# Fourth feed-forward part: both parts of the activations in one matmul of 512 columns, bank halves added by VectorE

## Chip, cores and metric

One core of a Trainium2 chip runs the whole program in one launch. The metric is the device time in microseconds, from one execution; of several executions the median is taken. The inputs are float32.

## The reference, cut to what matters

The program computes two layers of a first network (feed-forward, mixer, feed-forward in each) on 256 latent and 256 context tokens, and then two layers of a second network on the 256 latent tokens. The change touches only the second feed-forward of layer 1, the fourth of the program, which has the latent tokens alone:

```python
D_MODEL = 1024; D_FF = 2816; MACARON_WEIGHT = 0.5

def swiglu(x, w_gu, w_down):
    gate, up = jnp.split(x @ w_gu, 2, axis=-1)
    return (jax.nn.silu(gate) * up) @ w_down

def ffn_sublayer(x, shift, scale, gate, w_gu, w_down, g, b):
    y = swiglu(modulate(x, shift, scale), w_gu, w_down)
    return deepnorm_residual(x, MACARON_WEIGHT * gate * y, g, b)   # layer_norm(ALPHA * x + ...)
```

## The kernel before

Activations lie transposed: partitions are features, 128 at a time (`KD` = 8 tiles of X, `KF` = 22 tiles of the hidden H), and columns are tokens, `T` = 512 in the first three feed-forward parts, `L` = 256 in the fourth.

A float32 product is made from operands of a rounded type (fp32r). Weights and activations are each split in two: an upper part, which is the value rounded by a copy on ScalarE, and a lower part, the rest, by a subtraction on VectorE or GpSimd. For each tile of 128 x 128 weights, three matmuls are added in one PSUM bank: upper weights by upper X (L1947), lower weights by upper X (L1948), upper weights by lower X (L1950). Each has its own load of weights into TensorE. With n = 256 a matmul has 256 columns, and only half of the bank is used.

Weights come in one stream from DRAM, in chunks of 1024 columns (512 KB), into a ring of three slots. Half a chunk, 512 columns or four tiles, is the unit of the split: ScalarE's `split_hi` (L2292, its copy is on L2296) and VectorE's `split_lo` (L2539, L2542) fill one of `NSPL` = 4 pairs of buffers in `spl`. `split_hi` of a half waits until TensorE has used the half that lay in the same buffer, four before. In the parts up to the second network VectorE makes all lower parts of weights; GpSimd makes those of H (`dual`, ScalarE's part on L2300, GpSimd's on L3023).

One generator, `order`, yields the steps of the whole program in one order, and each engine runs through it and emits those that it has a function for. So the queue of each engine is this order, and an instruction that waits holds all that follow on its engine. `take` (L357), called for each weight tile, starts a new half when one is used up, and `splits_ahead` (L374) then puts into the order the splits of the half three ahead. `linear` (L428) goes over the k tiles of one output; after each fourth tile (k % 4 == 3) it may pump a step of a background generator: in this part `ada_vec` (L2556, its instruction on L2566), 16 product-sums on VectorE for the modulation vectors of the last norm, which end before m = KF - 4. In each second of four tiles (k % 4 == 1) it takes one step from `trickle`, here the eight `ln_update` of ScalarE (L2358) that the norm before has left.

`ffn` (L818) first makes gate and up for m = 0 and 1 side by side, beside the norm (`side_by_side`). Then for m = 2 to 21 it calls `linear` for gate (8 tiles, two halves) and for up (8 tiles, two halves), and yields `glu`: ScalarE takes silu of the gate bank into a temporary tile (L2335), VectorE multiplies it by the up bank (L2626), and `dual` splits the product into H. The eight down outputs follow, of 22 tiles each, with `residual` (L2615): X + gate column times bank, on VectorE (L2620). A load of ScalarE's table for the square root stands between up and down.

Of the kernel before, what the change touches and what calls it, by code (L numbers as in the profile page):

```python
# [15 lines left out]
KD = D // 128  # L16
# [217 lines left out]
def build(nc, nch, W, PRM, CST, XT, MT, OUT, stage="all"):  # L234
    ctx = ExitStack()
    with ctx:
# [34 lines left out]
        def R(a, n):  # L271
            return bigr[:, a:a + n]

        def two(ap):
            return ap.rearrange("p (s t) -> p s t", s=2)
# [63 lines left out]
        def order():  # L339
# [87 lines left out]

            def linear(key, w, src, n):  # L428
                bank, free, bi = banks.get()
                for k, (hi, lo, need) in enumerate(src):  # L430
                    tile = yield from take(w(k))
                    yield "linear", key, bank, free, k, len(src), tile, (hi, lo), need, n
                    if k % 4 == 1 and trickle:
                        yield trickle.pop(0)
                    if k % 4 == 3 and pos["auto"]:
                        i, steps, of = pos["auto"]
                        pos["auto"] = i + 1, steps, of
                        yield from pump((i + 1) * steps // of - i * steps // of)
                yield from run_later()
                return bank, bi  # L440
# [261 lines left out]

            def residual(key, bank, bi, k, n, gate, sums, xneed):
                u = new()
                yield "residual", u, k, n, bank, gate[0], [key, gate[1]], xneed
                banks.give(bi, ("res_x", u))

                def squares():
                    return sums.add(Xt[k][:, 0:n], [("res_x", u)], k == KD - 1)

                if n == L and k < KD - 1:
                    later.append(squares)
                else:
                    yield from squares()
# [103 lines left out]
            def ffn(f, n, xs, ms, ln, nxt, early=(), late=(), free=()):  # L818
# [22 lines left out]
                for m in range(KF):  # L841
# [5 lines left out]
                    else:  # L847
                        (kg, ku), (wg, wu) = gate_up(m)
                        bg, ig = yield from linear(kg, wg, src, n)
                        bu, iu = yield from linear(ku, wu, src, n)  # L850
                    t, free, i = tmps.get()
                    yield "glu", f, m, t[:, 0:n], bg[:, 0:n], bu[:, 0:n], free
                    banks.give(ig, ("silu", f, m))
                    banks.give(iu, ("glu", f, m))
                    h = yield from dual(t[:, 0:n], H[m][0], H[m][1], [("glu", f, m)])
# [16 lines left out]
                for k in range(KD):  # L872
                    if f == 3 and k < 4:
                        yield from scaled_later(1, MN1, [("mem_v", 0)], (2 * k, 2 * k + 1), srcm)
                    b, bi = yield from linear(("down", f, k), tile_of("ffn_w_down", (l, j), 128 * k), [(H[m][0], H[m][1], [hs[m]]) for m in range(KF)], n)
                    yield from residual(("down", f, k), b, bi, k, n, gate, sums, xs[k])
                pos["auto"] = None
# [1045 lines left out]
        def tensor_program(pe, w):  # L1923
# [16 lines left out]
            def linear(key, bank, free, k, nk, tile, x, need, n):  # L1940
# [9 lines left out]
                finish(pe.matmul(out, hi, x[1], start=False, stop=k == nk - 1), tile, key if k == nk - 1 else None)  # L1950

            def linear_hi(key, bank, free, tile, x, need, n):
                w.all(free, done)
# [308 lines left out]
            def index_heads(l, heads, need, IDX):  # L2262
# [9 lines left out]
            run({f.__name__: f for f in (  # L2272
                tables, linear, linear_hi, linear_lo, by_token, ada, ada_raw, ada_turn, colsum, square_sum, warm, spread, gate_columns, tail_columns, turn_kv,
                gram, gate_rows, unit_turn, q_decay, level_p, level_u, u_values, w_keys, scan_v, scan_s, scan_own, head_turn,
# [3 lines left out]
        def scalar_program(act, w):  # L2278
# [49 lines left out]
            def first_scale(k):  # L2328
                w.wait_ge(*done("first_mod", k))
                act.activation(Xt[k], Xt[k], ACTF.Copy, scale=ALPHA).then_inc(*sig("x_scaled", k))  # L2330

            def glu(f, m, t, bg, bu, free):
# [163 lines left out]
            def index_heads(l, heads, need, IDX):  # L2496
# [5 lines left out]
            run({f.__name__: f for f in (  # L2502
                tables, start, cond_silu, split_hi, dual, evacuate, ada_row, square, root, deviation, sqrt_table, first_scale, glu, ln_mod, ln_shift, ln_update,
                gates_in, gates_exp, gates_ratio, short_conv, conv_silu, conv_glu, z_silu, tail_columns, turn_kv, decay, unit_turn, q_decay,
# [3 lines left out]
        def vector_program(dve, w):  # L2508
# [105 lines left out]

            def residual(u, k, n, bank, gt, need, xneed):  # L2615
                w.all(need, done)
                w.all(xneed, done)
                for s, a, b in halves(n):
                    x = Xt[k][:, a:b]
                    ins = dve.scalar_tensor_tensor(x, bank[:, a:b], gt[:, k, s:s + 1], x, MUL, ADD)  # L2620
                ins.then_inc(*sig("res_x", u))

            def glu(f, m, t, bg, bu, free):
# [373 lines left out]
            def final(k, r, key):  # L2997
# [4 lines left out]
            run({f.__name__: f for f in (  # L3002
                tables, start, split_lo, dual, ada_turn, ada_vec, ada_mod, acc_dve, moments, inverse, norm_cols, gate_cols, residual, glu, first_mod, ln_sub, ln_mul,
                ln_mod, alpha_cols, ln_gain, gates_in, gates_exp, gates_ratio, gates_series0, gates_series1, gates_series2, gates_scan, gates_back,
# [151 lines left out]
```

## Time and profile before

| | us |
|---|---|
| median of 3 runs | 2625.61 |
| lowest, highest | 2621.83, 2629.3 |
| profiled execution, its own time | 2627.34 |
| span of the profiled execution | 2625.6 |
| busy in the span: TensorE matmul | 2505.6 (95%) |
| weight loads into TensorE | 2172.5 (83%) |
| VectorE | 1728.2 (66%) |
| ScalarE | 1215.8 (46%) |
| GpSimd | 666.5 (25%) |
| granted TensorE clock, mean | 0.984 of full |

PE is TensorE's matmul, PEld its weight load (which goes on beside matmuls), DVE VectorE, ACT ScalarE, POOL GpSimd. The span runs from the first to the last instruction. Times in the rows below are microseconds from its start unless marked otherwise. L and a number is a line of the kernel. Matmul records overlap: what counts for the pace is the distance between their starts.

### The profile page before, as it was taken

The page shows a single profiled execution, that of the slowest core. Times are in us where ns is not written, and L with a number is a line of the kernel's source. Part 1 is how long each engine was busy: PE and PEld are TensorE (multiplying, and loading weights), DVE is VectorE, ACT ScalarE, POOL GpSimd, SP SyncE. Part 2 cuts the span into 40 slices and gives each one's busy share as a digit, 9 for nine tenths or more (in the row PEclk, how much of TensorE's full clock was granted, in tenths as well). Part 3 has the DMA queues.
Part 4 walks back from the last instruction along what each step waited for, and adds up shares of the span by engine and source line. Part 5 has one row for each costly group of instructions (what it writes and reads, how often), then busy time and mean ns, then how long its engine had stood idle before and what let it go on. Part 6 is the DMA issues. An engine that isn't in the chain of part 4 may idle for free.

```text
span 2625.6 us, 42978 instructions
## 1 busy us (share of the span) xinstructions
PE 2505.6 (95%) x16456; PEld 2172.5 (83%) x16456; DVE 1728.2 (66%) x3436; ACT 1215.8 (46%) x2307; POOL 666.5 (25%) x602
## 2 busy tenths in 40 slices
PE   8999999997879999999999999999999999999998
PEld 5777887886777887888888887789998899999998
DVE  5786487898876687356764456676663476746766
ACT  4223324752153523324433325656555568555684
POOL 1101022002313211112111122121135543655435
PEclk9999999998999999999999999999999999999999
DMA  7554352220001455433453442237544444444444
GB/s 276 173 188 150 138 186 89 73 88 10 3 1 65 168 177 176 137 132 124 157 176 133 156 147 74 97 105 246 192 158 144 138 152 145 169 145 145 153 137 145
DMA packets 119324, 359.05 MB, mean 137 GB/s; under 512 B 13136, under 2 KB 15312, under 8 KB 118736
## 3 DMA queue, kind: packets, MB, share of 16 engines
q1 hardware_dynamic: 119120, 356.30, 39.8%
q8 instruction: 131, 2.15, 0.3%
q14 instruction: 73, 0.60, 0.1%
HBM read 355.20 MB, written 1.05 MB: 136 GB/s over the span
## 4 chain that ended last, share of the span: by engine, by line
PE 71%; DVE 11%; ACT 6%; issue 4%; DMA 4%; POOL 2%; SPq 0%; DVEq 0%; POOLq 0%; ACTq 0%
PE ps L1947 20%; PE ps L1950 20%; PE ps L1948 19%; DMA ring<-w_stream 4%; ACT spl L2296 2%; DVE work L2566 2%; DVE spl L2542 1%; DVE big L2566 1%; PE ps L2011 1%; DVE big L2760 1%; PE ps L2204 1%; PE ps L1972 1%; PE ps L1974 1%; PE ps L1973 1%; PE ps L2241 1%
## 5 line engine op out<-in xcount | busy, mean ns | idle before, releaser
L1947 PE MATMUL ps<-bigr,spl 128*128 128x256 f32 (+1 forms) x3850 | 1310.3, 340 | 31.9 <-DVE spl L2542 23.7
L1950 PE MATMUL ps<-bigr,spl 128*128 128x256 f32 (+1 forms) x3850 | 1291.0, 335 | 3.4 <-POOL bigr L3023 3.1
L1948 PE MATMUL ps<-bigr,spl 128*128 128x256 f32 (+1 forms) x3850 | 1288.3, 335 | 0.0
L2542 DVE TENSOR_TENSOR spl<-ring,spl 128x512 fp32r<-128x512 f32 x838 | 659.5, 794 | 587.4 <-ACT spl L2296 583.8
L2296 ACT ACTIVATE spl<-ring 128x512 fp32r<-128x512 f32 x1024 | 629.3, 627 | 752.1 <-PE ps L1950 504.5
L1947 PEld LDWEIGHTS ps<-bigr,spl 128*128 128x128 f32 x3850 | 732.5, 190 | 130.7 <-DVE spl L2542 30.5
L1950 PEld LDWEIGHTS ps<-bigr,spl 128*128 128x128 f32 x3850 | 732.1, 190 | 84.3 <-POOL bigr L3023 10.2
L1948 PEld LDWEIGHTS ps<-bigr,spl 128*128 128x128 f32 x3850 | 733.0, 190 | 73.2 <-issue 1.7
L3023 POOL TENSOR_TENSOR bigr<-work,bigr 128x512 fp32r<-128x512 f32 (+1 forms) x200 | 209.3, 1050 | 920.0 <-ACT bigr L2300 919.8
L3018 POOL TENSOR_TENSOR spl<-ring,spl 128x512 fp32r<-128x512 f32 x186 | 252.4, 1358 | 275.7 <-ACT spl L2296 275.0
L2300 ACT ACTIVATE bigr<-work 128x512 fp32r<-128x512 f32 (+1 forms) x224 | 117.0, 525 | 263.1 <-DVE work L2626 167.3
L3027 POOL TENSOR_TENSOR work<-work,X 128x512 f32<-128x512 f32 (+1 forms) x36 | 40.9, 1135 | 227.3 <-DVE X L2620 227.3
L2566 DVE CUSTOM_DVE_ANT_0 big<-big,prm 128x512 f32<-128x512 f32 x128 | 97.2, 759 | 0.0
L2566 DVE CUSTOM_DVE_ANT_0 big<-big,small 128x512 f32<-128x512 f32 x128 | 97.2, 759 | 0.0
L2760 DVE SCALAR_TENSOR_TENSOR big<-big,prm 128x512 f32<-128x512 f32 x120 | 95.8, 839 | 0.0
L2626 DVE TENSOR_TENSOR work<-work,ps 128x512 f32<-128x512 f32 (+1 forms) x88 | 54.4, 618 | 41.4 <-PE ps L1950 27.7
L2566 DVE CUSTOM_DVE_ANT_0 work<-big,small 128x512 f32<-128x512 f32 x96 | 78.4, 817 | 0.0
L2315 ACT ACTIVATE work<-X 128x256 f32<-128x256 f32 (+1 forms) x72 | 36.3, 507 | 85.3 <-DVE X L2620 74.7
L3027 POOL TENSOR_TENSOR work<-work 128x512 f32<-128x512 f32 (+1 forms) x47 | 62.3, 1325 | 48.5 <-ACT work L2315 48.5
L2566 DVE CUSTOM_DVE_ANT_0 work<-big,prm 128x512 f32<-128x512 f32 x96 | 74.3, 774 | 0.0
L1972 PE MATMUL ps<-spl,bigr 128*128 128x512 f32 (+1 forms) x128 | 51.6, 403 | 1.6 <-DVE spl L2542 1.0
L2935 DVE TENSOR_TENSOR big<-big,work 128x256 f32<-128x256 f32 x52 | 30.4, 585 | 28.3 <-POOL big L3075 27.8
(312 smaller groups left out, 2377.9 us busy)
## 6 DMA issues: line engine op xcount, KB each, us to landing
ring<-w_stream SPq DMA_DIRECT2D x512, 512.0 KB, 3.3
big<-w_stream SPq DMA_DIRECT2D x280, 256.0 KB, 3.0
big<-w_stream SPq DMA_DIRECT2D x16, 512.0 KB, 10.8
X<-x_t SPq DMA_DIRECT2D x2, 1024.0 KB, 13.6
cst<-consts SPq DMA_DIRECT2D x1, 1537.5 KB, 9.0
X<-mem_t SPq DMA_DIRECT2D x1, 1024.0 KB, 5.9
out_t<-X SPq DMA_DIRECT2D x8, 128.0 KB, 2.1
prm<-params SPq DMA_DIRECT2D x1, 252.5 KB, 2.6
```

Of the source, the lines that this page charges most:

```text
L1947: pe.matmul(out, hi, x[0], start=k == 0, stop=False)
L1948: pe.matmul(out, lo, x[0], start=False, stop=False)
L1950: finish(pe.matmul(out, hi, x[1], start=False, stop=k == nk - 1), tile, key if k == nk - 1 else None)
L1972: pe.matmul(outs[i], src[0][:, a:b], hi, start=k == 0, stop=False)
L2296: act.activation(hi_half(h), raw_half(h), ACTF.Copy).then_inc(*sig("hi", h))
L2300: act.activation(hi, raw, ACTF.Copy).then_inc(*sig("dhi", u))
L2542: dve.tensor_tensor(lo_half(h), raw_half(h), hi_half(h), SUB).then_inc(*sig("lo", h, by="lo_dve"))
L2566: ins = dve.tensor_tensor_reduce(slot if s == conds - 1 else wk[7 + j % 2], slot, crow[s][h], 1.0, start, MUL, ADD, col)
L2760: ins = dve.scalar_tensor_tensor(two(CF[m]), YP[m][:, :, j:j + 256], a, two(CF[m]), MUL, ADD)
L3018: pool.tensor_tensor(lo_half(h), raw_half(h), hi_half(h), SUB).then_inc(*sig("lo", h, by="lo_pool"))
L3023: pool.tensor_tensor(lo, raw, hi, SUB).then_inc(*sig("dlo", u, by="dlo_pool"))
L3027: ins = pool.tensor_copy(dst, src) if copy else pool.tensor_tensor(dst, dst, src, ADD)
```

## The change

For n = L (only the fourth part has it) `linear` is told `wide`. A step `linear_wide` then gives TensorE two matmuls for a weight tile instead of three. The first has the upper weights, and as its moving operand both parts of X, 256 columns each, taken from two places that lie a fixed distance apart (`both_parts`); it fills both halves of the bank, the product with the upper part in columns 0 to 255 and that with the lower part in 256 to 511. The second, with the lower weights and the upper part of X, adds to the first half. For the last k the order of the two is turned round.

The halves of the bank have then to be added. For the gate VectorE does it with a reduction (`gate_sum`) into the temporary tile, and ScalarE's silu works there in place; the step stands right behind gate's `linear`, before up's. For up a second reduction (`up_sum`) writes into the other half of the same tile, waits for itself, and the product follows. In down the residual becomes two instructions on X, one for each half of the bank, with a wait between them, for k = 0 to 6; k = 7 stays as it was. m = 0 and 1 of gate and up also stay.

In the diff, hunks that only list the new functions for an engine are left out.

```diff
--- before.py
+++ after.py
@@ -271,6 +271,13 @@
         def R(a, n):
             return bigr[:, a:a + n]
 
+        def sides(ap):
+            return ap.rearrange("p (s t) -> p s t", s=2)
+
+        def both_parts(hi, lo):
+            step = lo.offset - hi.offset
+            return sides(bigr[:, hi.offset:hi.offset + 2 * step])[:, :, 0:hi.shape[1]]
+
         def two(ap):
             return ap.rearrange("p (s t) -> p s t", s=2)
 
@@ -425,11 +432,11 @@
                     yield from pump()
 
 
-            def linear(key, w, src, n):
+            def linear(key, w, src, n, wide=False):
                 bank, free, bi = banks.get()
                 for k, (hi, lo, need) in enumerate(src):
                     tile = yield from take(w(k))
-                    yield "linear", key, bank, free, k, len(src), tile, (hi, lo), need, n
+                    yield "linear_wide" if wide else "linear", key, bank, free, k, len(src), tile, (hi, lo), need, n
                     if k % 4 == 1 and trickle:
                         yield trickle.pop(0)
                     if k % 4 == 3 and pos["auto"]:
@@ -700,9 +707,9 @@
                 yield "gate_cols", u, gt[:, :, 0:n], mods[l][:, i, :, 0:n], half, mod_ready(l, i)
                 return gt, ("gatec", u)
 
-            def residual(key, bank, bi, k, n, gate, sums, xneed):
+            def residual(key, bank, bi, k, n, gate, sums, xneed, wide=False):
                 u = new()
-                yield "residual", u, k, n, bank, gate[0], [key, gate[1]], xneed
+                yield "residual", u, k, n, bank, gate[0], [key, gate[1]], xneed, wide
                 banks.give(bi, ("res_x", u))
 
                 def squares():
@@ -846,12 +853,20 @@
                         (bg, ig), (bu, iu) = first[2 * m:2 * m + 2]
                     else:
                         (kg, ku), (wg, wu) = gate_up(m)
-                        bg, ig = yield from linear(kg, wg, src, n)
-                        bu, iu = yield from linear(ku, wu, src, n)
-                    t, free, i = tmps.get()
-                    yield "glu", f, m, t[:, 0:n], bg[:, 0:n], bu[:, 0:n], free
-                    banks.give(ig, ("silu", f, m))
-                    banks.give(iu, ("glu", f, m))
+                        bg, ig = yield from linear(kg, wg, src, n, n == L)
+                        if n == L:
+                            t, free, i = tmps.get()
+                            yield "gate_sum", f, m, t[:, 0:n], bg, free
+                            banks.give(ig, ("gate_sum", f, m))
+                        bu, iu = yield from linear(ku, wu, src, n, n == L)
+                    if n == L and 2 * m >= len(first):
+                        yield "up_sum", f, m, t, bu
+                        banks.give(iu, ("up_sum", f, m))
+                    else:
+                        t, free, i = tmps.get()
+                        yield "glu", f, m, t[:, 0:n], bg[:, 0:n], bu[:, 0:n], free
+                        banks.give(ig, ("silu", f, m))
+                        banks.give(iu, ("glu", f, m))
                     h = yield from dual(t[:, 0:n], H[m][0], H[m][1], [("glu", f, m)])
                     tmps.give(i, h)
                     hs.append(h)
@@ -872,8 +887,8 @@
                 for k in range(KD):
                     if f == 3 and k < 4:
                         yield from scaled_later(1, MN1, [("mem_v", 0)], (2 * k, 2 * k + 1), srcm)
-                    b, bi = yield from linear(("down", f, k), tile_of("ffn_w_down", (l, j), 128 * k), [(H[m][0], H[m][1], [hs[m]]) for m in range(KF)], n)
-                    yield from residual(("down", f, k), b, bi, k, n, gate, sums, xs[k])
+                    b, bi = yield from linear(("down", f, k), tile_of("ffn_w_down", (l, j), 128 * k), [(H[m][0], H[m][1], [hs[m]]) for m in range(KF)], n, n == L and k < KD - 1)
+                    yield from residual(("down", f, k), b, bi, k, n, gate, sums, xs[k], n == L and k < KD - 1)
                 pos["auto"] = None
                 yield from drain()
                 if not nxt:
@@ -1949,6 +1964,21 @@
                 w.all(need, done)
                 finish(pe.matmul(out, hi, x[1], start=False, stop=k == nk - 1), tile, key if k == nk - 1 else None)
 
+            def linear_wide(key, bank, free, k, nk, tile, x, need, n):
+                if k == 0:
+                    w.all(free, done)
+                for step, u in need:
+                    w.wait_ge(*done("dhi", u))
+                hi, lo = weights(tile)
+                if k < nk - 1:
+                    w.all(need, done)
+                    pe.matmul(sides(bank), hi, both_parts(*x), start=k == 0, stop=False)
+                    finish(pe.matmul(bank[:, 0:n], lo, x[0], start=False, stop=False), tile, None)
+                else:
+                    pe.matmul(bank[:, 0:n], lo, x[0], start=False, stop=False)
+                    w.all(need, done)
+                    finish(pe.matmul(sides(bank), hi, both_parts(*x), start=False, stop=True), tile, key)
+
             def linear_hi(key, bank, free, tile, x, need, n):
                 w.all(free, done)
                 for step, u in need:
@@ -2328,6 +2358,10 @@
             def first_scale(k):
                 w.wait_ge(*done("first_mod", k))
                 act.activation(Xt[k], Xt[k], ACTF.Copy, scale=ALPHA).then_inc(*sig("x_scaled", k))
+
+            def gate_sum(f, m, t, bg, free):
+                w.wait_ge(*done("gate_sum", f, m))
+                act.activation(t, t, ACTF.Silu).then_inc(*sig("silu", f, m))
 
             def glu(f, m, t, bg, bu, free):
                 w.wait_ge(*done("gate", f, m))
@@ -2612,13 +2646,29 @@
                 w.all(need, done)
                 dve.tensor_scalar(gt, mod, half, None, MUL).then_inc(*sig("gatec", u))
 
-            def residual(u, k, n, bank, gt, need, xneed):
+            def residual(u, k, n, bank, gt, need, xneed, wide):
                 w.all(need, done)
                 w.all(xneed, done)
+                if wide:
+                    x = Xt[k][:, 0:n]
+                    link(dve.scalar_tensor_tensor(x, bank[:, n:2 * n], gt[:, k, 0:1], x, MUL, ADD))
+                    linked()
                 for s, a, b in halves(n):
                     x = Xt[k][:, a:b]
                     ins = dve.scalar_tensor_tensor(x, bank[:, a:b], gt[:, k, s:s + 1], x, MUL, ADD)
                 ins.then_inc(*sig("res_x", u))
+
+            def gate_sum(f, m, t, bg, free):
+                w.wait_ge(*done("gate", f, m))
+                w.all(free, done)
+                dve.tensor_reduce(t, bg.rearrange("p (s t) -> p t s", s=2), AXX, ADD).then_inc(*sig("gate_sum", f, m))
+
+            def up_sum(f, m, t, bu):
+                w.wait_ge(*done("up", f, m))
+                dve.tensor_reduce(t[:, L:T], bu.rearrange("p (s t) -> p t s", s=2), AXX, ADD).then_inc(*sig("up_sum", f, m))
+                w.wait_ge(*done("up_sum", f, m))
+                w.wait_ge(*done("silu", f, m))
+                dve.tensor_tensor(t[:, 0:L], t[:, 0:L], t[:, L:T], MUL).then_inc(*sig("glu", f, m))
 
             def glu(f, m, t, bg, bu, free):
                 w.wait_ge(*done("silu", f, m))
```

## Rows read from the trace of the kernel before

**Rows 1.** The page, its first part: engine, busy us, share, instructions.

```profile
PE 2505.6 (95%) x16456; PEld 2172.5 (83%) x16456; DVE 1728.2 (66%) x3436; ACT 1215.8 (46%) x2307; POOL 666.5 (25%) x602
```

**Rows 2.** Windows: length; PE, PEld, DVE, ACT, POOL busy (instructions); clock; DMA share, GB/s.

```profile
1860.00:1880.00 20.00, 20.00 (x169) 20.00 (x168) 11.36 (x18) 10.93 (x22) 2.95 (x4) 1.00 0.54 179
1920.00:1940.00 20.00, 20.00 (x170) 20.00 (x168) 12.31 (x18) 9.80 (x18) 7.17 (x8) 1.00 0.55 184
```

**Rows 3.** TensorE in order of time: 32 matmuls, then 10: start, duration.

```profile
1819.76 0.28 PE L1948 MATMUL ps<-bigr,spl 128*128 128x256 f32 x1
...
1823.48 0.28 PE L1950 MATMUL ps<-bigr,spl 128*128 128x256 f32 x1
...
1399.94 0.39 PE L1947 MATMUL ps<-bigr,spl 128*128 128x512 f32 x1
...
1401.98 0.39 PE L1947 MATMUL ps<-bigr,spl 128*128 128x512 f32 x1
```

**Rows 4.** Waits between 1777 and 1952: us in total, times, longest.

```profile
ACT spl L2296 <- PE ps L1950: 51.9, 68, 0.9
```

**Rows 5.** VectorE's groups, whole span: busy us, mean ns, idle before.

```profile
L2910 DVE TENSOR_REDUCE small<-ps 128x1 f32<-128x512 f32 x16 | 11.0, 686 | 4.9 <-PE ps L2204 4.9
L2626 DVE TENSOR_TENSOR work<-work,ps 128x256 f32<-128x256 f32 x22 | 9.2, 419 | 2.9 <-ACT work L2335 1.6
L2718 DVE TENSOR_TENSOR_SCAN work<-big 32x512 f32<-32x512 f32 x1 | 1.2, 1216 | 0.0
L2620 DVE SCALAR_TENSOR_TENSOR X<-ps,small,X 128x256 f32<-128x256 f32 x80 | 35.5, 479 | 12.3 <-PE ps L1950 11.8
```

**Rows 6.** VectorE in order of time, an instruction that waits for the one before.

```profile
1764.44 0.41 DVE L2644 TENSOR_TENSOR X<-X,ps 128x256 f32<-128x256 f32 x1
1764.89 0.41 DVE L2649 TENSOR_SCALAR work<-X,small 128x256 f32<-128x256 f32 x1
```

**Rows 7.** VectorE in order of time, from three places in gate and up.

```profile
1789.38 0.74 DVE L2566 CUSTOM_DVE_ANT_0 big<-big,prm 128x512 f32<-128x512 f32 x1
1790.06 0.07 DVE L2566 DVE_READ_ACCUMULATOR2_ANT small<- 128x1 f32 x1
1790.06 1.28 DVE L2542 TENSOR_TENSOR spl<-ring,spl 128x512 fp32r<-128x512 f32 x2
1791.26 0.41 DVE L2626 TENSOR_TENSOR work<-work,ps 128x256 f32<-128x256 f32 x1
...
1871.39 0.42 DVE L2626 TENSOR_TENSOR work<-work,ps 128x256 f32<-128x256 f32 x1
1872.82 1.41 DVE L2542 TENSOR_TENSOR spl<-ring,spl 128x512 fp32r<-128x512 f32 x2 [1.00 <-ACT spl L2296]
...
1888.67 0.42 DVE L2626 TENSOR_TENSOR work<-work,ps 128x256 f32<-128x256 f32 x1
```

**Rows 8.** ScalarE in order of time, behind the product at 1871.39.

```profile
1871.85 0.42 ACT L2300 ACTIVATE bigr<-work 128x256 fp32r<-128x256 f32 x1 [1.00 <-DVE work L2626]
1872.17 1.28 ACT L2296 ACTIVATE spl<-ring 128x512 fp32r<-128x512 f32 x2
```

**Rows 9.** Groups between 1777 and 1888, ScalarE: busy us, mean ns, idle before.

```profile
L2335 ACT ACTIVATE work<-ps 128x256 f32<-128x256 f32 x20 | 7.3, 365 | 0.0
L2358 ACT ACTIVATE X<-X,small 128x256 f32<-128x256 f32 x8 | 4.7, 589 | 0.0
L2290 ACT ACTIVATE big<-big 128x512 f32<-128x512 f32 x2 | 1.1, 620 | 0.0
```

**Rows 10.** The chain that ended last, behind m = 1: start, us, what.

```profile
1775.13 0.43 DVE work L2626
...
1776.56 0.82 DVE spl L2542
1777.42 0.39 PE ps L1947
```

**Rows 11.** ScalarE in order of time, between up and down.

```profile
1889.57 1.28 ACT L2326 ACT_TABLE_LOAD   x1
```

More of the change, by code:

```diff
@@ L2272, in tensor_program @@
             run({f.__name__: f for f in (
-                tables, linear, linear_hi, linear_lo, by_token, ada, ada_raw, ada_turn, colsum, square_sum, warm, spread, gate_columns, tail_columns, turn_kv,
+                tables, linear, linear_wide, linear_hi, linear_lo, by_token, ada, ada_raw, ada_turn, colsum, square_sum, warm, spread, gate_columns, tail_columns, turn_kv,
                 gram, gate_rows, unit_turn, q_decay, level_p, level_u, u_values, w_keys, scan_v, scan_s, scan_own, head_turn,
@@ L2502, in scalar_program @@
             run({f.__name__: f for f in (
-                tables, start, cond_silu, split_hi, dual, evacuate, ada_row, square, root, deviation, sqrt_table, first_scale, glu, ln_mod, ln_shift, ln_update,
+                tables, start, cond_silu, split_hi, dual, evacuate, ada_row, square, root, deviation, sqrt_table, first_scale, gate_sum, glu, ln_mod, ln_shift, ln_update,
                 gates_in, gates_exp, gates_ratio, short_conv, conv_silu, conv_glu, z_silu, tail_columns, turn_kv, decay, unit_turn, q_decay,
@@ L3002, in vector_program @@
             run({f.__name__: f for f in (
-                tables, start, split_lo, dual, ada_turn, ada_vec, ada_mod, acc_dve, moments, inverse, norm_cols, gate_cols, residual, glu, first_mod, ln_sub, ln_mul,
+                tables, start, split_lo, dual, ada_turn, ada_vec, ada_mod, acc_dve, moments, inverse, norm_cols, gate_cols, residual, gate_sum, up_sum, glu, first_mod, ln_sub, ln_mul,
                 ln_mod, alpha_cols, ln_gain, gates_in, gates_exp, gates_ratio, gates_series0, gates_series1, gates_series2, gates_scan, gates_back,
```

## The prediction

> **What bounds the kernel now.** I read the page first: TensorE is busy in 95% of the span [rows 1]. The feed-forward part f = 3 runs, by its first and last instructions, from about 1762 to 1952 us. A table of windows laid over it shows TensorE full in every microsecond, at the full granted clock (1.00, the 2.4 GHz level), and the weight loads full too, VectorE at 57 to 62% and ScalarE at 49 to 55% [rows 2]. Next comes the pace. In order of time, matmuls of 256 columns start 31 steps in 3.72 us, 120 ns apart; matmuls of 512 columns, in an earlier part, start 9 steps in 2.04 us, 227 ns apart [rows 3]. 256 more columns cost 107 ns, so each matmul carries 13 ns that do not go with columns. Today a weight tile is 3 x 120 = 360 ns, a half (four tiles, one split) 1.44 us, a pair (gate and up of one m, 16 tiles) 5.76 us.
>
> Last I read the two engines that feed TensorE. By the waits, ScalarE's splits wait for TensorE (68 times, 51.9 us), because a split needs the buffer that was used four halves ago [rows 4]: the feeders are ahead and TensorE sets the pace. The lead is about three halves.
>
> **The change on TensorE.** Per tile 227 + 120 = 347 ns instead of 360, so 13 ns less. Wide tiles: 20 pairs (m = 2 to 21; m = 0 and 1 are issued side by side in the old form) x 16 = 320, and 7 x 22 = 154 in down. If TensorE stayed the bound, this would be 474 x 13.3 = 6.3 us. No row shows two strided runs of 256 as moving data; from both sides, a tile could cost 333 ns (the fixed part gone from both matmuls, which the 120 ns beside a weight load that is always busy leaves open) or 360 ns (nothing gained). I take 347, the two measured paces. The rows give 120 and 227 ns; the Trainium skill ("TensorE: Matmul & The Clock Gate", its sections on back-to-back gaps) has columns / 2.4 plus about 2.5 ns, which would be 109 and 216 ns, and a gain of 2.5 ns a tile, 1 us in all. The measured steps do not agree with it.
>
> **The change on VectorE and ScalarE.** Per pair VectorE now does two reductions of 512 PSUM elements to 256. The nearest row is the reduction of 512 PSUM elements at 0.69 us; below, the 256-element operation that reads PSUM is 0.42, above, the slowest operation on 512 elements is the scan at 1.22 [rows 5]. I take 0.69, because it has the same operation, source and number of elements read. The Trainium skill ("VectorE: DVE Perf Modes", Rules for kernel authors) calls the reduction on a hot path the slowest VectorE operation, to be avoided. The row has it level with a subtraction of the same 512 elements (0.69), so its rate is not the trouble here; that it is there at all, in the queue below, is.
>
> VectorE's sum per pair is 4 splits, 2 reductions, a product, and up to m = 17 about one product-sum of the modulation vector: 4 x 0.61 + 2 x 0.61 + 0.34 + 0.68 = 4.7 us of start-to-start time, still under the 5.55 us (16 x 347 ns) TensorE would need. But sums of busy time are not the limit. The queues are in order, and what matters is how they now alternate. The order for a pair, by the order written in the program, with u2 the second half of this pair's up weights and g1', g2', u1' halves of the next:
>
> VectorE: low part of u2, low g1', **gate_sum**, low g2', low u1', **up_sum**, product.
> ScalarE: high u2, high g1', **silu** (now behind gate_sum), high g2', high u1', high part of H (behind the product).
>
> Before, silu read the bank itself, and the only crossing back from VectorE to ScalarE was the product. Now there are two, and the high parts queued behind each have to wait. I follow one round, from the start of up_sum at 0:
> - reduction 0.69, wait for itself 0.04 (a multiply that feeds the next instruction: start 1764.44, 0.41 long, next start 1764.89) [rows 6], product 0.42: done 1.15.
> - ScalarE starts the high part of H 0.03 later, and the next split 0.32 after that: 1.51 (1871.85 to 1872.17) [rows 8]. High u2 done 2.14, high g1' 2.79 (two take 1.28).
> - VectorE: low u2 from 2.17 to 2.98, low g1' done 3.58 (the two take 1.41 [rows 7]; the first is 0.82 [rows 10], beside GpSimd's low part of H). gate_sum starts 0.08 before that end, 3.50 to 4.19.
> - ScalarE: silu at 4.22, next split 0.33 later at 4.55 (I take silu from SBUF as the row of the same size from PSUM, 0.37 [rows 9]); high g2' done 5.18, high u1' 5.83.
> - VectorE: low g2' from 5.21, low u1' from 5.86, up_sum 0.61 after it (two splits and the next start: 1790.06, 1791.26) [rows 7].
>
> The round closes at 6.47 us. TensorE needs 5.55 and needed 5.76. The same round before is product 0.42, 0.03, 0.32, four high parts 2.58, 0.03 and 0.61 to the next product: 4.0 us, which is why it was hidden. The lead is soon used up: if up_sum starts as TensorE ends up, low g2' is done at 5.9 and TensorE wants it five halves on, at 6.9. That is the tightest place, and each round takes 0.9 of it. From then TensorE waits twice a round, for u2 and for g2'.
>
> The modulation product-sums (16, ended before m = 18) are queued on VectorE between the splits, never in its two idle places (behind the product and behind gate_sum), so each adds its 0.68 us (1789.38 to 1790.06) [rows 7]: 16 x 0.68 = 10.9 us. They cost nothing before. The eight ln_update of ScalarE (0.59 us) fall in m = 2 and 3 between its splits, with two silu of condition rows (0.62 us) behind them [rows 9]. One between two high parts makes the second some 0.5 us later, of which VectorE's own work hides a part: I estimate 0.6 in m = 2, 0.75 in m = 3 and 0.5 for the two silu, 1.9 together.
>
> That such a round does hold TensorE up is already to be seen: after m = 1, where ScalarE had been held by a table load, the chain goes product 1775.13, high, low 1776.56, TensorE 1777.42 [rows 10].
>
> **Sum for gate and up.** From the product of m = 1 (1775.13) to up_sum of m = 21: 20 x 6.47 = 129.4, less 0.73 because m = 1 has no reduction, plus 10.9, plus 1.9 = 141.5, so at 1916.6. TensorE is then 2.1 us ahead: low u2 done 2.98, its four tiles 1.39, so 4.37 in a round of 6.47. It ends up at 1914.5, against 1888.67 now, where the last product starts as the last matmul ends [rows 7]: +25.8 us.
>
> **Down.** The first three halves are split by then. The fourth waits behind the product, the high part and now also a table load of 1.28 us [rows 11] and its 0.2 us operation: 1.51 + 1.48 + 0.63 + 0.03 + 0.69 = 4.3 us after up_sum. TensorE, through three halves at 2.2, waits 2.1 us, and 0.2 for the half before: +2.3. The residuals get a second operation of 0.48 us [rows 5] and a wait of 0.04, seven times. VectorE has splits behind them, but is busy 62% here and three halves ahead, and a residual of 1.0 us plus a split 0.69 is under 4.2, so this costs nothing; if the cover were gone it would be 7 x 0.52 = 3.6 us. The last residual (k = 7) stays as it is. TensorE gains 154 x 13.3 ns = 2.05 us here. The other edits (a bank given back later, a temporary tile kept longer, both parts of H awaited before the first matmul) have seven other banks, two other tiles and H values made at least a pair earlier as cover. Loads of weights follow the splits and become rarer per microsecond.
>
> Sum: 25.8 + 2.3 - 2.05 = +26 us. The profiled execution took 2627.34 (span 2625.6 and 1.7 around it), which gives 2653.4; it is 1.7 above the median of the runs, 2625.61, and from that the forecast is 2652 us.
>
> **Rivals.**
> - *A: TensorE stays the bound.* The queues never close on each other; the gain is the 6.3 us above, 2619 us. For it: VectorE's sum of 4.7 is under 5.55. Against: the written order, and the round.
> - *B: faster.* The same, and the fixed part goes from both matmuls, 474 x 26.6 ns = 12.6 us: 2613 us. Its place is TensorE's tiles of f = 3; it decides only if the round is under 5.33 us, which would need both reductions to cost 0.1 us each or less. Nothing in the rows comes near.
> - *C: a milder chain.* A reduction at 0.42: the round is 5.93, the sum less 39 x 0.27 = 10.5 us: 2641 us.
> - *D: a slower reduction.* The two inputs of each sum lie 256 elements apart, and writing 256 results may cost more than writing one. At the scan's 1.22 the round is 7.53: 39 x 0.53 = 20.7 us more, 2673 us.
>
> [...]
>
> **Chances.** The forecast's chain at about 0.69 a reduction 0.60, C 0.15, D 0.14, A 0.08, B 0.03. The forecast's own range is 2643 to 2663. The range for 8 in 10 takes in C and most of D: 2636 to 2674. A measurement of this kernel tells 0.3% (8 us) from no change. Faster by more is B: 0.03. Within it: A and the mildest end of C: 0.09. Slower: 0.88.
>
> **What would show it.** In the profile after: matmuls of 512 columns 227 ns apart from the next in f = 3; TensorE no longer full between 1780 and 1915, with idle time ended by VectorE's splits, twice a pair; up_sum 6.5 us apart after m = 17 and some 7.2 before; gate_sum and up_sum at 0.69 us; waits of ScalarE for gate_sum; ScalarE's splits no longer waiting for TensorE. In down TensorE is full again after its first halves and each k takes 7.63 instead of 7.92 us. Wrong would be a TensorE that is full throughout (A or B), or rounds of another length with the reduction at another price (C, D), or waits for DMA of weights in place of splits.

## The result, and the profile after

| | before | after |
|---|---|---|
| median, us | 2624.47 (4 runs, 2621.83 to 2629.3) | 2653.38 (4 runs, 2649.45 to 2658.14) |
| profiled execution: its own time, span | 2627.34, 2625.6 | 2658.14, 2656.3 |
| ratio | | 1.0104, 95% interval 1.009 to 1.0118 |

The change makes the kernel 29 us slower (24 to 31 by the interval). The profiled execution after is the slowest of its four, so I measure inside the part: from the product of m = 1, the last step that both kernels share, to the last residual. That is 1775.13 to 1951.96 before, 176.8 us, and 1778.22 to 1980.96 after, 202.7 us: 25.9 us more. Of the other 4.8 us that the two spans differ by, 3.1 lie before this stretch and 1.7 behind it, where the instructions are the same. Over all the kernels below the product of m = 1 starts anywhere from 1770 to 1778 us, with no order in it, so I take them for spread between executions.

Windows of the kernel after, columns as in [rows 2]: gate and up while the product-sums of the modulation run, gate and up behind them, and down.

```profile
1780.00:1857.00 77.00, 64.55 (x338) 51.48 (x336) 53.39 (x97) 35.82 (x74) 7.33 (x10) 1.00 0.57 194
1857.00:1912.00 55.00, 48.83 (x259) 39.63 (x260) 38.59 (x69) 23.40 (x48) 5.91 (x8) 1.00 0.48 160
1930.00:1980.00 50.00, 50.00 (x304) 44.35 (x304) 33.14 (x52) 26.00 (x48) 16.00 (x18) 1.00 0.58 190
```

TensorE was full in [rows 2]; now it is at 84 and 89% in gate and up and full again in down, at a granted clock of 1.00 throughout. VectorE is at 69 and 70% in gate and up: no engine is full there. What holds the part is a chain over two of them, and VectorE and ScalarE in order of time show one whole round of it (start, duration, engine and line; L2576 is VectorE's split, L2664 gate_sum, L2668 up_sum, L2671 the product):

```profile
1911.96 0.68 DVE L2668 TENSOR_REDUCE work<-ps 128x256 f32<-128x512 f32 x1
1912.68 0.42 DVE L2671 TENSOR_TENSOR work<-work 128x256 f32<-128x256 f32 x1
1914.11 1.42 DVE L2576 TENSOR_TENSOR spl<-ring,spl 128x512 fp32r<-128x512 f32 x2 [1.01 <-ACT spl L2326]
1915.45 0.68 DVE L2664 TENSOR_REDUCE work<-ps 128x256 f32<-128x512 f32 x1
1917.14 1.29 DVE L2576 TENSOR_TENSOR spl<-ring,spl 128x512 fp32r<-128x512 f32 x2 [1.01 <-ACT spl L2326]
1918.35 0.69 DVE L2668 TENSOR_REDUCE work<-ps 128x256 f32<-128x512 f32 x1
```

```profile
1913.13 0.42 ACT L2330 ACTIVATE bigr<-work 128x256 fp32r<-128x256 f32 x1 [1.90 <-DVE work L2671]
1913.46 1.14 ACT L2326 ACTIVATE spl<-ring 128x512 fp32r<-128x512 f32 x2
1916.16 0.42 ACT L2364 ACTIVATE work<-work 128x256 f32<-128x256 f32 x1 [1.56 <-DVE work L2664]
1916.49 1.14 ACT L2326 ACTIVATE spl<-ring 128x512 fp32r<-128x512 f32 x2
```

Read across: when ScalarE works, VectorE waits (1.01 us, twice), and when VectorE works, ScalarE waits (1.90 and 1.56). Behind each wait stand two splits. Before, the product of VectorE was the only place where this happened [rows 7, 8], once in 5.76 us. The waits name it too (us in all, times, longest, from 1776 to 1982):

```profile
ACT bigr L2330 <- DVE work L2671: 41.6, 20, 2.6
ACT work L2364 <- DVE work L2664: 35.8, 20, 2.2
PEld ps L1975 <- DVE spl L2576: 29.2, 36, 1.5
ACT spl L2326 <- PE ps L1976: 20.2, 27, 0.9
PE ps L1975 <- DVE spl L2576: 18.8, 30, 1.1
```

ScalarE's splits, which waited for TensorE 51.9 us in [rows 4] (23.5 of them before 1889, in gate and up), do so for 20.2 on this line now, all of it in down, behind 1917. In gate and up they never do, and TensorE waits for VectorE's splits instead. The page's chain has VectorE at 15% of the span, where it had 11.

### The profile page after: what moved, and what is told of

Read it like the earlier page. It is cut to its first block, busy times and chain, and to the rows that moved or that the text cites. A ratio compares the mean times of both kernels' runs of the same rounds, so it can differ in the third digit from the quotient of the medians.

```text
span 2656.3 us, 42115 instructions
## 1 busy us (share of the span) xinstructions
PE 2515.3 (95%) x15982; PEld 2150.4 (81%) x15982; DVE 1753.3 (66%) x3483; ACT 1213.8 (46%) x2307; POOL 668.5 (25%) x602
## 4 chain that ended last, share of the span: by engine, by line
PE 65%; DVE 15%; ACT 7%; issue 6%; DMA 4%; POOL 2%; SPq 0%; DVEq 0%; POOLq 0%; ACTq 0%
PE ps L1962 17%; PE ps L1965 17%; PE ps L1963 17%; DMA ring<-w_stream 4%; ACT spl L2326 3%; DVE spl L2576 3%; DVE big L2600 2%; DVE work L2600 2%; PE ps L1975 1%; PE ps L2041 1%; DVE big L2810 1%; PE ps L2234 1%; PE ps L2002 1%; PE ps L2004 1%; PE ps L2003 1%
## 5 line engine op out<-in xcount | busy, mean ns | idle before, releaser
L1962 PE MATMUL ps<-bigr,spl 128*128 128x512 f32 (+1 forms) x3376 | 1176.3, 348 | 32.6 <-DVE spl L2576 24.6
L1965 PE MATMUL ps<-bigr,spl 128*128 128x512 f32 (+1 forms) x3376 | 1156.5, 343 | 3.5 <-POOL bigr L3073 3.2
L1963 PE MATMUL ps<-bigr,spl 128*128 128x512 f32 (+1 forms) x3376 | 1154.1, 342 | 0.0
L2576 DVE TENSOR_TENSOR spl<-ring,spl 128x512 fp32r<-128x512 f32 x838 | 658.2, 794 | 591.0 <-ACT spl L2326 588.2
L1962 PEld LDWEIGHTS ps<-bigr,spl 128*128 128x128 f32 x3376 | 641.3, 190 | 131.7 <-DVE spl L2576 30.9
L1965 PEld LDWEIGHTS ps<-bigr,spl 128*128 128x128 f32 x3376 | 641.3, 190 | 84.1 <-POOL bigr L3073 10.1
L1963 PEld LDWEIGHTS ps<-bigr,spl 128*128 128x128 f32 x3376 | 641.9, 190 | 73.5 <-issue 1.7
L1975 PE MATMUL ps<-bigr,spl 128*128 128x512 f32 x427 | 157.7, 406 | 20.8 <-DVE spl L2576 18.8
L1976 PE MATMUL ps<-bigr,spl 128*128 128x256 f32 x427 | 119.6, 280 | 0.0
L1975 PEld LDWEIGHTS ps<-bigr,spl 128*128 128x128 f32 x427 | 80.1, 188 | 47.9 <-DVE spl L2576 29.2
L1976 PEld LDWEIGHTS ps<-bigr,spl 128*128 128x128 f32 x427 | 80.6, 189 | 1.7
## 6 DMA issues: line engine op xcount, KB each, us to landing
big<-w_stream SPq DMA_DIRECT2D x16, 512.0 KB, 10.6
X<-x_t SPq DMA_DIRECT2D x2, 1024.0 KB, 13.5
```

The source lines that it names most:

```text
L1962: pe.matmul(out, hi, x[0], start=k == 0, stop=False)
L1963: pe.matmul(out, lo, x[0], start=False, stop=False)
L1975: pe.matmul(sides(bank), hi, both_parts(*x), start=k == 0, stop=False)
L1976: finish(pe.matmul(bank[:, 0:n], lo, x[0], start=False, stop=False), tile, None)
L2576: dve.tensor_tensor(lo_half(h), raw_half(h), hi_half(h), SUB).then_inc(*sig("lo", h, by="lo_dve"))
```

## Experiments

I name the theory Q: the two queues alternate in a round longer than TensorE's work. Its rivals are W, that VectorE has too much work, and P, that the wide matmuls themselves cost time. "Gate and up" is from the product of m = 1 to the last product or up_sum: 113.5 us before, 140.1 after.

The kernel before was run again beside each group of experiments, and its median moved: 2624.47 us beside the changed kernel, 2625.97 beside the first four below (no additions, gate_sum behind up, product-sums moved, both moves), and 2629.09 and 2628.79 beside the others. Each ratio is to the kernel before of its own group. Differences between medians of different groups can be off by these 4 to 5 us; gate and up, read within one trace, does not have this trouble.

**No additions.**

```diff
-                        if n == L:
-                            t, free, i = tmps.get()
-                            yield "gate_sum", f, m, t[:, 0:n], bg, free
-                            banks.give(ig, ("gate_sum", f, m))
...
-                    if n == L and 2 * m >= len(first):
+                    if False:
...
-                    yield from residual(("down", f, k), b, bi, k, n, gate, sums, xs[k], n == L and k < KD - 1)
+                    yield from residual(("down", f, k), b, bi, k, n, gate, sums, xs[k])
```

> Leaves out the additions of the bank halves (and with them the product with the lower part of X and H in wide tiles): the wide matmuls stay, silu and the product read only the first half of the bank, the residual is one instruction. Theory Q (the queues of VectorE and ScalarE alternate in too long a round): TensorE is the bound again and gains what its own tiles gain. In down of the changed kernel a wide tile takes 0.353 us against 0.360, so 474 x 0.007 = 3 us under before: 2621 us, f = 3 full on TensorE. Rival P (the wide matmul, or the wait for both parts ahead of it, is what costs): still near 2650. Rival W (VectorE has too much work): as Q here.

2622.74 us, 0.999 of before (0.998 to 0.9999), gate and up 111.6 us. Windows of it:

```profile
1860.00:1880.00 20.00, 20.00 (x116) 17.43 (x115) 11.38 (x19) 10.87 (x21) 2.21 (x3) 1.00 0.59 186
1920.00:1940.00 20.00, 20.00 (x116) 17.37 (x115) 11.52 (x17) 9.68 (x17) 3.94 (x5) 1.00 0.55 195
```

TensorE is full, with the wide matmuls in place. P falls: all the loss, and more, goes with the additions. The run does not tell Q from W, since both lose their cause.

**gate_sum and its silu behind up.**

```diff
                         bg, ig = yield from linear(kg, wg, src, n, n == L)
+                        bu, iu = yield from linear(ku, wu, src, n, n == L)
                         if n == L:
...
                             yield "gate_sum", f, m, t[:, 0:n], bg, free
                             banks.give(ig, ("gate_sum", f, m))
-                        bu, iu = yield from linear(ku, wu, src, n, n == L)
```

> Same instructions, gate_sum (and the silu behind it) moved from behind gate to behind up, next to up_sum. Q: one crossing from VectorE to ScalarE in a round instead of two. Round = 0.61 + 0.73 + 0.42 + 0.03 + 0.32 + 0.63 + 0.03 + 0.73 + 3 x 0.61 = 5.3 us without a product-sum of the modulation, 6.0 with one; TensorE needs 5.65. So rounds of 5.65 after m = 17, some 6.1 to 6.2 in the 12 or 13 pairs with product-sums, less the lead of 3 us: gate and up some 118 to 121 us instead of 140, the kernel 2628 (2623 to 2633). Rival W (the sum of VectorE's work): no change from the changed kernel, 2653, since the work is the same.

2634.15 us, 1.0026 of before (1.0015 to 1.0037), gate and up 122.7. The same instructions in another order give back 19 of 29 us (17.4 of 26.6 in gate and up), so W falls as a theory of amounts. The last five rounds, behind the product-sums, average 5.60 us. Both figures lie a little outside what was expected (2623 to 2633, and 118 to 121 for gate and up): one round took 7.9 us and another 6.2, and in each a split of ScalarE stood waiting for weights (2.2 and 1.2 us of 7.1 in all for DMA).

**Only silu moved on ScalarE, behind the two high parts.**

```diff
                     if n == L and 2 * m >= len(first):
+                        yield "gate_silu", f, m, t[:, 0:n]
                         yield "up_sum", f, m, t, bu
...
-            def gate_sum(f, m, t, bg, free):
+            def gate_silu(f, m, t):
                 w.wait_ge(*done("gate_sum", f, m))
                 act.activation(t, t, ACTF.Silu).then_inc(*sig("silu", f, m))
```

> The changed kernel with one ScalarE instruction moved: silu is queued behind the high parts of g2' and u1' instead of ahead of them. VectorE's order and all work stay. Q: the second crossing is gone, the round is 0.69 + 0.04 + 0.42 + 0.03 + 0.32 + 0.63 + 0.03 + 0.73 + 4 x 0.61 = 5.3 us (6.0 with a product-sum), so TensorE's 5.65 after m = 17 and gate and up some 122 to 125 us as with gate_sum moved; 2634 (2629 to 2638). Rival W (VectorE's amount of work, or where gate_sum stands on VectorE): as the changed kernel, 2653.

2632.25 us, 1.0014 of before (1.0001 to 1.0027), inside the range; gate and up 119.0, under the 122 to 125 expected. This is the sharpest of the runs: VectorE does what it did in the changed kernel, in its order, and one ScalarE instruction in a pair stands two places later. ScalarE in one round:

```profile
1889.40 0.42 ACT L2331 ACTIVATE bigr<-work 128x256 fp32r<-128x256 f32 x1 [1.60 <-DVE work L2672]
1889.73 1.14 ACT L2327 ACTIVATE spl<-ring 128x512 fp32r<-128x512 f32 x2
1891.04 0.63 ACT L2327 ACTIVATE spl<-ring 128x512 fp32r<-128x512 f32 x1 [0.17 <-PE ps L1981]
1892.50 0.63 ACT L2327 ACTIVATE spl<-ring 128x512 fp32r<-128x512 f32 x1 [0.83 <-PE ps L1977]
1893.04 0.40 ACT L2365 ACTIVATE work<-work 128x256 f32<-128x256 f32 x1
1895.05 0.42 ACT L2331 ACTIVATE bigr<-work 128x256 fp32r<-128x256 f32 x1 [1.60 <-DVE work L2672]
```

In this round, behind the product-sums, silu does not wait, two splits wait for TensorE again as in [rows 4], and the round is 5.65 us, TensorE's own. Over the whole of gate and up silu's waits fell from 35.8 us (20 times) to 6.9 (12 times). Rounds with one product-sum are 5.95: there the round of the queues, 5.28 in the first two behind the product-sums, plus 0.67 for the product-sum, is over TensorE's. That is what is left of the loss.

**up_sum's reduction twice.**

```diff
+                link(dve.tensor_reduce(t[:, L:T], ..., AXX, ADD))
+                linked()
                 dve.tensor_reduce(t[:, L:T], ..., AXX, ADD).then_inc(*sig("up_sum", f, m))
```

> The changed kernel with up_sum's reduction done twice, same result. Q: the reduction lies on the round, 0.69 us and 0.04 for the wait: rounds of 6.39 become 7.1 after m = 17, gate and up 140.1 + 20 x 0.72 = 154.5 us. W (VectorE's throughput, with idle time to fill): VectorE has 1.9 us idle in a round of 6.4 and would take the extra 0.7 in it, rounds unchanged.

One run, 2666.65 us; gate and up 153.7, 13.5 more. The first reductions of the last two up_sums and the doubled one between (VectorE):

```profile
1920.03 0.69 DVE L2668 TENSOR_REDUCE work<-ps 128x256 f32<-128x512 f32 x1
1920.75 0.69 DVE L2670 TENSOR_REDUCE work<-ps 128x256 f32<-128x512 f32 x1
...
1927.12 0.69 DVE L2668 TENSOR_REDUCE work<-ps 128x256 f32<-128x512 f32 x1
```

The round is 7.09 us, 0.70 over 6.39. VectorE has idle time in every round, yet an instruction on the round costs its whole length.

**The product-sums in VectorE's idle places.**

```diff
-                    if k % 4 == 3 and pos["auto"]:
+                    if k % 4 == 3 and pos["auto"] and not wide:
...
                             yield "gate_sum", f, m, t[:, 0:n], bg, free
                             banks.give(ig, ("gate_sum", f, m))
+                            yield from gap(2)
...
                     hs.append(h)
+                    if n == L and 2 * m >= len(first):
+                        yield from gap(2)
```

`gap(2)` pumps what two halves would have pumped.

> The changed kernel with the 16 product-sums of the modulation pumped right behind gate_sum and right behind the product, where VectorE waits 1.0 us for ScalarE in each round, instead of between splits. Q: they hide; all rounds are 6.4 us, gate and up 140 - 16 x 0.68 = 129 us, the kernel 11 us under the changed one: 2642. W: no change, 2653.

2644.82 us, 8.6 under the changed kernel, gate and up 135.4 where 129 was expected. Most rounds were 6.37 to 6.39 as forecast, but two were 8.4 and some 7, and ScalarE waited 6.4 us for weight loads. This run alone leaves open whether the product-sums hide; a later kernel, with their loads issued one product-sum later, answers it.

**Both moves together.** The edits of the two, but pumped behind the product alone.

```diff
                     hs.append(h)
+                    if n == L and 2 * m >= len(first):
+                        yield from gap(4)
```

> Both: gate_sum behind up, and the product-sums pumped behind the product, once a pair. Q: round 5.3 us, with the product-sums in the 1.0 us gap (when two come in one gap, 0.4 us more), under TensorE's 5.65: TensorE is the bound in nearly all of f = 3. 3 us under before, less up to 2 at the start of the part and the start of down: 2622 to 2624. W: 2653, as the work is that of the changed kernel.

2639.31 us, 1.006 of before (1.0039 to 1.0082), gate and up 127.0: a miss by 16 us, and worse than gate_sum behind up alone. Most rounds are 5.64 or less, but three are between 9.3 and 10.4. One of the long ones, ScalarE (L2334 its split) and then what SyncE's queue waited for (in all, times, longest; L1927 is the load of a product-sum's weights):

```profile
1797.83 0.62 ACT L2334 ACTIVATE spl<-ring 128x512 fp32r<-128x512 f32 x1
1802.45 1.15 ACT L2334 ACTIVATE spl<-ring 128x512 fp32r<-128x512 f32 x2 [4.01 <-DMA ring<-w_stream]
```

```profile
SPq L1927 <- DVE small L2608: 36.7, 10, 5.6
```

The load for a product-sum takes the slot that the one before has just left, so SyncE stands behind VectorE, and the weights of the ring stand behind SyncE. The longest of these waits is 5.6 us here; with single product-sums in both idle places it was 7.0, and 3.8 in the changed kernel.

**These loads issued one product-sum later.**

```diff
-                        if work_ and any(x is not None for x in slots.free):
+                        if work_ and sum(x is not None for x in slots.free) >= (2 if p == 6 else 1):
```

> The kernel with gate_sum behind up and the product-sums behind the product, and the loads of the product-sums' weights issued one product-sum later, so that SyncE's queue no longer stands behind a product-sum of VectorE while weights for the ring are due. If that queue made the two stalls of 4 to 5 us and ScalarE's 14.8 us of waits for DMA in the run without this: rounds 5.65 with few exceptions, waits for DMA under 5 us, gate and up 114 to 117 us, the kernel 2622 to 2625. If the order of the queues was not the cause: as that run, 2639.

2627.24 us, 0.9996 of before (0.9986 to 1.0005), over the 2622 to 2625 expected, where the kernel before had 2629.09 beside it; gate and up 115.3 and 4.8 us of waits for DMA, both as expected. The queue's waits fell:

```profile
SPq L1927 <- DVE small L2608: 16.1, 6, 3.3
```

The same edit on the kernel with the product-sums in both idle places:

> The changed kernel with the product-sums in the two idle places behind gate_sum and behind the product, and their loads issued one later. If SyncE's queue took 2 to 3 us of what the same move without the later loads should have given (it gave 8.6 of 11): rounds of 6.38 throughout, gate and up 20 x 6.38 - 0.73 + 2 = 129 us, the kernel 11 us under the changed one, 2642 against 2653. If the product-sums' cost was not their place on the round: no better than the move alone, 2645.

2642.0 us, 1.005 of before (1.0032 to 1.0067), gate and up 129.2, 10.9 under the changed kernel's 140.1; every round from m = 5 on is 6.37 to 6.39, and ScalarE no longer waits for DMA. So the 16 product-sums cost what they did by where they stood. By the rounds it is 10.6 us: in the changed kernel the ten rounds with one are 7.05 and the three with two are 7.73, against 6.39. The other 0.3 of the 10.9 is the difference of the first rounds.

**Both parts side by side.** Down alone wide, with H so laid out; and the kernel with both moves and lagged loads (2627.24 us), with H and X so laid out (the edit for X and those that undo the wide form of gate and up are not shown).

```diff
+                if n == L:
+                    H = [(R(2 * KD * T + 2 * m * n, n), R(2 * KD * T + (2 * m + 1) * n, n)) for m in range(KF)]
```

> Only down is wide, gate and up are as before; and the two parts of an H tile lie side by side, so that the wide matmul's moving operand is one run of 512 columns. If the two runs 5632 elements apart are what makes a wide tile 353 ns where the paces of before gave 347: 0.347 us a tile, 7.63 us between residuals. If it is something else (the full bank, the two sizes in turn): 0.353, 7.77 us. Gate and up as before (5.76 a pair): residuals cost nothing on TensorE; the kernel 1 to 2 us under before in either case.

> The same with both parts side by side everywhere in f = 3 (H, and X for gate and up). If runs apart cost 6 ns a tile: pair 5.55 us, 2 to 3 us under the kernel with lagged loads, 2620. Otherwise the same as that. The round of the queues, 5.3 us, is still the shorter, but by little.

2626.98 us (one run) and 2627.46 us (1.0 of before, 0.9988 to 1.0011): nothing gained. TensorE in down, ten tiles after the change, then five with down alone wide and H side by side:

```profile
1945.64 0.40 PE L1975 MATMUL ps<-bigr,spl 128*128 128x512 f32 x1
...
1949.18 0.28 PE L1978 MATMUL ps<-bigr,spl 128*128 128x256 f32 x1
```

```profile
1929.80 0.40 PE L1973 MATMUL ps<-bigr,spl 128*128 128x512 f32 x1
1930.15 0.40 PE L1973 MATMUL ps<-bigr,spl 128*128 128x512 f32 x1
...
1931.56 0.40 PE L1973 MATMUL ps<-bigr,spl 128*128 128x512 f32 x1
```

A tile is 354 ns in the first and 352 in the second (five in 1.76 us): the layout is not the cause. Nor is the full bank or the turn of sizes by itself, for the same instructions also ran at the forecast's pace. In the changed kernel the second output of down has 21 tiles in 7.29 us, 347 ns each, with nothing else in their place:

```profile
1926.35 0.40 PE L1975 MATMUL ps<-bigr,spl 128*128 128x512 f32 x1
...
1933.64 0.28 PE L1978 MATMUL ps<-bigr,spl 128*128 128x256 f32 x1
```

With down alone wide TensorE has no wait between 1889 and 1951 us, so down's second residual instruction costs it nothing.

No version beat the kernel before by what can be told with some certainty; the one closest to it that computes everything is level with it.

## Why the prediction was right

The forecast was 2652 us against 2653.4 measured, and its steps can be set against the trace one by one. The mechanism held; that the total came within 1.4 us is in part luck, since terms that were off cancel.

- **The round.** Forecast 6.47, measured 6.39. Crossing by crossing from up_sum: product 0.72 (0.73), high part of H 1.17 (1.18), split 1.50 (1.51), low u2 2.15 (2.17), gate_sum 3.49 (3.50), silu 4.20 (4.22), split 4.53 (4.55), low g2' 5.18 (5.21). The rest is ScalarE's second split: two take 1.14 when nothing holds the second, where the row I used had 1.28 [rows 8].
- **The reduction.** 0.685 and 0.679 us (20 each) for 256 sums of two elements 256 apart: the row with one result [rows 5] was the right one, and rivals C and D fall. The kernel with it doubled shows that it is paid in full.
- **The product-sums.** Forecast 16 x 0.68 = 10.9, measured 10.6 by the rounds; moving them gave 10.9 (140.1 to 129.2).
- **The first two rounds.** ScalarE's ln_update and the two silu were to cost 1.9 us; the rounds of m = 2 and 3 are 0.7 and 1.7 over the others, 2.5 together.
- **Gate and up.** Forecast 141.5 to up_sum of m = 21, measured 140.1: the rounds gave 1.6 less and the product-sums 0.3 less, the first two rounds 0.6 more. TensorE ended 1.9 us ahead of it (2.1): down's first matmul starts at 1916.50. The part was to lose 25.8 us up to there and lost 24.8.
- **Down.** Forecast +0.3 in all; measured 64.5 us from that start to the last residual against 63.3 before: +1.2. Before the fourth half TensorE was idle for 1.8 us, and with the slow start of the matmuls at both waits this makes 2.1 of the 2.3 forecast. But the tile was mis-sized: it saved 0.9 of the 2.05 us.
- **The tile.** Forecast 347 ns from two paces measured apart, measured 353 in most of the part, so half of the 13 ns saved. In down that is 154 x 6 = 0.9 us. An output of down was to take 7.63 us; one of them did (7.64), the later ones take 7.77. Had TensorE stayed the bound, the gain would have been 3 us and not 6.3, as the kernel without additions shows: rival A's price was off.
- **B's sum.** It takes the fixed 13 ns off once, though it says that they go from both matmuls: a tile would then be 320 ns and not 333, the gain 474 x 40 ns = 19 us and the kernel 2607 us. No run shows a tile under 347 ns in steady running.
- **A and W.** VectorE's sum of start-to-start time was under TensorE's, as forecast, and it did not help; three kernels with the same work in another order (gate_sum behind up, silu alone moved, product-sums moved with later loads) settle it.

The sum for the part was 26.1 and is 25.9, with 1.0 less in gate and up and 0.9 more in down. The 29 between the medians holds 3 us more, within the interval and without a place in the trace; the kernel before now has 2624.47 with a fourth run, where the forecast started from 2625.61.

What I had not seen is the third queue. The prediction priced the moved splits and left SyncE with a sentence; in the changed kernel that was near enough (2.9 us of waits for DMA, against 3.1 before). In the kernels with the product-sums moved ScalarE waited 6.4 and 14.8 us for DMA, and none and 4.8 once their loads were issued later. With gate_sum behind up and with silu moved it waited 7.1 and 7.3; no run shows whether the same loads caused those.

## What to carry to other kernels

Follow one round of the in-order queues of engines that feed each other, with start-to-start times, before adding up busy time: two reductions that fit into idle time cost 26 us, most of it because one of them put a second crossing between two queues: moving a single instruction two places took 21 of the 26.6 us in gate and up back. A crossing costs everything queued behind it; put it where the queue behind it is not yet due, and put independent work right behind the instruction that the other engine waits for. When such a move misses, look next at the queue that issues the loads.

## What the runs showed of the hardware

- A matmul of 512 columns followed by one of 256, each with a weight load of its own, takes 352 to 354 ns for the two in most of the wide stretches, where each kind among its own took 227 and 120. Parts side by side instead of 5632 elements apart made no difference. In other stretches the same pair takes 347 ns, the sum of the two paces: 21 tiles of down's second output (1926.35 to 1933.64 in the changed kernel), and eight tiles right behind a wait (1892.08 to 1894.85 in the kernel with both parts side by side). What decides between the two paces stays open; bank, sizes and layout are the same in both.
- The reduction of 512 PSUM elements on VectorE costs the same whether it writes 256 results (0.685 us) or one (0.686 [rows 5]).
